# First feed-forward of a two-block kernel: every input weight group stationary, the first two taken by turns for each piece of x

## The chip, the cores and the metric

One NeuronCore of a Trainium2 chip runs the whole kernel. The metric is the device time of one execution in microseconds; lower is better. Everything is fp32. Matrix products are split into high and low parts (`hi*hi + hi*lo + lo*hi`, parts rounded to the fp32r format), so each weight has to be rounded (`w_hi`) and its remainder taken (`w_lo`) before TensorE (PE) may use it.

## The reference

Two blocks on one sequence of 256 tokens of width 1024. The change touches only the first feed-forward, which stands first in the program:

```python
h = _swiglu(_rms_norm(x, ffn1_pre_norm), ffn1_w_in, ffn1_w_out)
x = x + 0.5 * _rms_norm(h, ffn1_post_norm)

def _swiglu(x, w_in, w_out):
    g, u = jnp.split(x @ w_in, 2, axis=-1)      # w_in: 1024 x 5632
    return (jax.nn.silu(g) * u) @ w_out         # w_out: 2816 x 1024
```

After it come a token mixer, a second feed-forward, two more mixers and a final norm. They are computed as before.

## The kernel before, in words

**Weights.** All weights come as one stream of groups of 128 x 2048 fp32 (1 MB). SyncE (SP) loads each into one of `RING = 6` slots of `raw`, as soon as PE has finished with the slot's old group (`RELEASE`). ScalarE (ACT) rounds a group into `w_hi` (`round_to(n)`: all groups below n). VectorE (DVE) then takes the remainder into `w_lo` (`low_to(n)`), in place of `raw`. DVE can't start on a group before ACT has ended it (`hi_done`), and PE can't before DVE has (`lo_done`).

**First feed-forward, input products.** They are 22 groups. The first four are "straight": x is stationary and 512 weight columns stream, in the layout tokens x columns. The results are transposed afterwards (`hidden_transposes`). `opening()` takes these groups in pieces as they land. The other 18 are "chunks": a group holds 128 gate columns and the 128 up columns that belong to them. The weights are stationary and `xT` streams, 32 matmuls to a chunk, by turns of 512 columns (high and low of x with `w_hi`) and 256 columns (`w_lo`). The result is already transposed. A chunk fills one of two pairs of PSUM banks, `acc[:, c % 2]`, first half gate, second half up.

**What a chunk asks of ACT and DVE.** For chunk n, ACT does in this order: copy half of the gate (`gate_second_part`), round a later weight group, SiLU (`chunk_silu`), copy half of up (`up_second_part`), round the product (`chunk_round`). DVE does: sum the gate, scale it by the row of 1/rms of x (`chunk_gate`), take the remainder of a later weight group (`low_to`), sum up (`chunk_up`, which signals `up_summed`), product, remainder of the product (`chunk_low`). Each engine works strictly in the order written. PE begins chunk c only when `up_summed` says that chunk c - 2, the last user of the banks, is summed. In both engines' code the loop over the chunks decides which weight group is handled beside which chunk.

**Norm of x.** The first norm is applied behind the product. Before, ACT squares x by tokens, DVE takes the reciprocals and makes a diagonal, and PE turns it into the row `rstd0_row`. `rates()` is some small mathematics for the later mixers: 20 columns, 20 instructions of DVE and one exponential of ACT.

**Behind it.** `f1_out` follows on PE without a gap. It begins when the last chunk but one is summed; its second token tile begins when the last one is.

Of the kernel before, what the change touches and what calls it, by code (L numbers as in the profile page):

```python
# [59 lines left out]
ACC_READERS = {"f1_in": "V" * 2, "f1_out": "V", "mix_in": "AVVVVVVVVAAAA", "na_out": "V", "mix_out": "V",  # L60
# [7 lines left out]
FILL_COUNTS = [("f1_in", 2), ("t1", 4), ("rq", 2), ("rk", 2), ("rs", 4), ("rp", 4),  # L68
# [4 lines left out]
SPLIT_COUNTS = [("f1_in", 2), ("t1", 4), ("yret", 4), ("merged", 4), ("t2", 4),  # L73
# [5 lines left out]
WARM = 4  # L79
STRAIGHT, CHUNKS = 4, 18  # L80
CHUNKS_BEFORE = {"f1_in": 0, "f2_in": CHUNKS}
# [5 lines left out]
for _name, _n in STAGES:  # L87
    for _g in range(_n):
        if _name in CHUNKS_BEFORE and _g >= STRAIGHT:
            RELEASE.append(("chunk", CHUNKS_BEFORE[_name] + _g - STRAIGHT + 1))  # L90
# [34 lines left out]
def build(nc, first_in, weights, x_turned_in, x_in, gain0_in, gains, rot_in, colmask_in, dist_in, decay_in, lam_in, bias_in, gate_w_in,  # L125
          gate_b_in, conv_a_in, conv_ab_in, conv_b_in, out):
    with ExitStack() as ctx:
# [68 lines left out]
        gate_c = at("gate_c", [P, 2, S], F32, area + 51200)  # L196
        prod_c = at("prod_c", [P, 2, S], F32, area + 53248)

        warm = at("warm", [P, P + 256], F32, area + 63488)
        rstd0_diag = at("rstd0_diag", [P, T, P], F32, area + 65536)  # L200
        rstd0_row = at("rstd0_row", [P, S], F32, area + 66560)

# [57 lines left out]
        warm_set = sem("warm_set")  # L260
        rstd0_ready = sem("rstd0_ready")
        rstd0_diag_ready = sem("rstd0_diag_ready")
        rstd0_row_full = sem("rstd0_row_full")
        rstd0_row_ready = sem("rstd0_row_ready")
        half_hi, half_lo = sem("half_hi"), sem("half_lo")
# [22 lines left out]
        x_landed = [sem(f"x_landed{t}") for t in range(T)]  # L288
        turned_landed = [sem(f"turned_landed{j}") for j in range(KD // 2)]
        unit_landed = [sem(f"unit_landed{j}") for j in range(2)]  # L290
        unit_hi, unit_lo = sem("unit_hi"), sem("unit_lo")
        first_hi, turned_hi = sem("first_hi"), sem("turned_hi")
        part_landed = [sem(f"part_landed{g}") for g in range(1, 3)]
# [80 lines left out]

        def pair_bank(b):

            return acc[:, b % 4 // 2, b % 2]
# [5 lines left out]
        def _(sp):  # L383
# [14 lines left out]
            for j in range(2):  # L398
                sp.dma_start(raw[:, 0, j * UNIT:(j + 1) * UNIT], first_in[j]).then_inc(unit_landed[j], 16)
            load_turned(1)  # L400
            sp.dma_start(raw[:, 0, 2 * UNIT:].rearrange("p (j n) -> p j n", j=2),
                         first_in[2:4].rearrange("j p n -> p j n")).then_inc(landed[0], 16)
            for j in range(2, KD // 2):
                load_turned(j)
            for g in range(1, 3):
                for half, done in enumerate((part_landed[g - 1], landed[g])):
                    part = slice(half * GROUP // 2, (half + 1) * GROUP // 2)
                    sp.dma_start(raw[:, g, part], weights[g - 1][:, part]).then_inc(done, 16)
            sp.dma_start(raw[:, 3, :], weights[2]).then_inc(landed[3], 16)
            for t in range(T):  # L410
                sp.dma_start(x[:, t], x_in[t * P:(t + 1) * P, :]).then_inc(x_landed[t], 16)
            for g in range(4, RING):
                sp.dma_start(raw[:, g, :], weights[g - 1]).then_inc(landed[g], 16)
            for g in range(RING, NG):
# [3 lines left out]
                sp.dma_start(raw[:, g % RING, :], weights[g - 1]).then_inc(landed[g % RING], 16)  # L418
# [12 lines left out]
        def _(pool):  # L431
# [15 lines left out]
            pool.wait_ge(landed[3], 16)  # L447
            for dst, src in ((colmask, colmask_in), (conv_a, conv_a_in), (conv_ab, conv_ab_in),
                             (conv_b, conv_b_in), (gate_b, gate_b_in), (rot, rot_in)):
                pool.dma_start(dst[:], src).then_inc(consts_in, 16)  # L450
            pool.dma_start(logit[:, 0:2 * RH], decay_in.partition_broadcast(P)).then_inc(consts_in, 16)
            pool.dma_start(logit[:, 2 * RH:], lam_in).then_inc(consts_in, 16)
# [18 lines left out]
            def mask_bias(s):  # L471
                pool.wait_ge(bias_in_s[s % 2], 16 * (s // 2 + 1))
                if s == 0:
                    pool.wait_ge(consts_in, 16 * 8)
# [39 lines left out]
        def _(act):  # L514
# [69 lines left out]
            def opening():  # L584

                def token_sums(t):
                    act.wait_ge(x_landed[t], 16)
                    step(a.activation(prod[:].rearrange("p a t n -> p (a t n)"), x[:, t], ACT.Square,
                                      accum_out=sumsq[:, 2 + t:3 + t]))
                    a.activation(std[:, 2 + t:3 + t], sumsq[:, 2 + t:3 + t], ACT.Sqrt, bias=eps1[:], scale=1.0 / DM)\  # L590
                        .then_inc(pre_std, 1)

# [7 lines left out]
                def round_unit(j):  # L600
                    act.wait_ge(unit_landed[j], 16)
                    part = slice(j * UNIT, (j + 1) * UNIT)
                    a.activation(w_hi[:, 0, part], raw[:, 0, part], ACT.Copy).then_inc(unit_hi, 1)

                def round_half(g, half):
                    part = slice(half * GROUP // 2, (half + 1) * GROUP // 2)
# [17 lines left out]
                for t in range(T):  # L624
                    token_sums(t)
# [362 lines left out]
        def _(dve):  # L988
# [150 lines left out]
            def swiglu(which):  # L1139
# [64 lines left out]
                if g0 == 0:  # L1204
                    rates()
# [1018 lines left out]
```

## Time and profile before

| | |
|---|---|
| median of 3 runs | 888.8 us (888.74 to 888.95) |
| the profiled execution's own time | 888.69 us, span 887.0 us |
| PE busy | 879.6 us, 99% |
| DVE, ACT busy | 625.0 us (70%), 489.4 us (55%) |
| granted TensorE clock, mean | 0.999 of 2.4 GHz |
| DMA | 169.89 MB, mean 192 GB/s |

The span runs from the first to the last instruction; the 1.7 us that the execution's own time has more lie around it. In the trace, matmul rows start at even steps when PE is full, so the distance between two starts is the time of what lies between them.

### The profile page before, as it was taken

The numbers are of one execution on the slowest core, as the hardware profiler recorded it, in microseconds if no ns is written. First come the engines' busy times: TensorE is split into PE (matmuls) and PEld (weight loads), VectorE is DVE, ScalarE is ACT, GpSimd is POOL, SyncE is SP. The second block draws the span as 40 slices with busy tenths as digits, with TensorE's granted clock in tenths as the row PEclk, the third lists the DMA queues.
The fourth block names the chain that finished last, engine by engine and source line by source line (L and its number), as shares of the span: only waits on it lengthen the run. The fifth ranks groups of instructions, "written<-read, shape, count | busy, mean of one in ns | idle before, by whom it ended". The sixth has DMA issues, their size and how long they took to land.

```text
span 887.0 us, 11473 instructions
## 1 busy us (share of the span) xinstructions
PE 879.6 (99%) x4628; PEld 752.3 (85%) x4628; DVE 625.0 (70%) x808; ACT 489.4 (55%) x661; POOL 64.4 (7%) x89
## 2 busy tenths in 40 slices
PE   9999999999999999999999999999999999999997
PEld 7888888888888888888888888888999888888886
DVE  6887776467767656577577777446979857888872
ACT  6865564445444556446565555435887644555551
POOL 2000000003021110000000000000390000000000
PEclk9999999999999999999999999999999999999999
DMA  9955555455753444455655555546534456555521
GB/s 352 368 188 191 191 189 199 147 190 179 282 198 127 180 168 173 184 190 190 237 190 190 191 190 190 189 182 251 184 106 181 151 187 254 190 190 191 190 95 48
DMA packets 26948, 169.89 MB, mean 192 GB/s; under 512 B 3616, under 2 KB 3664, under 8 KB 7952
## 3 DMA queue, kind: packets, MB, share of 16 engines
q1 hardware_dynamic: 24368, 161.23, 50.3%
q0 software_dynamic: 2240, 7.66, 2.5%
q8 instruction: 37, 0.61, 0.3%
q10 hardware_dynamic: 288, 0.27, 0.1%
q14 instruction: 15, 0.12, 0.0%
HBM read 167.05 MB, written 1.05 MB: 190 GB/s over the span
## 4 chain that ended last, share of the span: by engine, by line
PE 97%; DVE 1%; ACT 1%; issue 0%; ACTq 0%
PE acc L1839 15%; PE acc L1642 15%; PE acc L1640 15%; PE acc L1641 15%; PE acc L2101 8%; PE acc L1841 7%; PE acc L2103 4%; PE acc L1655 2%; PE acc L1883 2%; PE acc L2053 2%; PE acc L2054 2%; PE acc L2052 2%; PE aux L2037 1%; PE aux L1764 1%; PE acc L1885 1%; PE aux L1641 1%
## 5 line engine op out<-in xcount | busy, mean ns | idle before, releaser
L996 DVE TENSOR_TENSOR w_lo<-raw,w_hi 128x2048 fp32r<-128x2048 f32 x147 | 336.8, 2300 | 89.9 <-ACT w_hi L522 89.5
L522 ACT ACTIVATE w_hi<-raw 128x2048 fp32r<-128x2048 f32 x145 | 275.7, 1911 | 62.6 <-DMA raw<-weights 62.4
L1839 PE MATMUL acc<-xT,w_hi 128*128 128x512 f32 x576 | 200.4, 394 | 0.0
L1841 PE MATMUL acc<-xT,w_lo 128*128 128x256 f32 x576 | 159.7, 277 | 0.0
L1839 PEld LDWEIGHTS acc<-xT,w_hi 128*128 128x128 f32 x576 | 108.0, 188 | 25.0
L1640 PE MATMUL acc<-w_hi,xT 128*128 128x512 f32 x312 | 124.0, 398 | 0.0
L1642 PE MATMUL acc<-w_hi,xT 128*128 128x512 f32 x312 | 121.8, 390 | 0.0
L1641 PE MATMUL acc<-w_lo,xT 128*128 128x512 f32 x312 | 121.5, 390 | 0.0
L2101 PE MATMUL acc<-xT,w_hi 128*128 128x512 f32 x320 | 111.3, 394 | 0.0
L1841 PEld LDWEIGHTS acc<-xT,w_lo 128*128 128x128 f32 x576 | 108.2, 188 | 0.0
L2103 PE MATMUL acc<-xT,w_lo 128*128 128x256 f32 x320 | 88.7, 277 | 0.0
L2101 PEld LDWEIGHTS acc<-xT,w_hi 128*128 128x128 f32 x320 | 60.0, 188 | 13.8
L1642 PEld LDWEIGHTS acc<-w_hi,xT 128*128 128x128 f32 x312 | 58.6, 188 | 12.6
L1640 PE MATMUL acc<-w_hi,hT_hi 128*128 128x512 f32 x176 | 68.7, 390 | 0.0
L1640 PEld LDWEIGHTS acc<-w_hi,xT 128*128 128x128 f32 x312 | 58.6, 188 | 11.8 <-issue 0.6
L1642 PE MATMUL acc<-w_hi,hT_lo 128*128 128x512 f32 x176 | 68.5, 389 | 0.0
L1641 PE MATMUL acc<-w_lo,hT_hi 128*128 128x512 f32 x176 | 68.5, 389 | 0.0
L1641 PEld LDWEIGHTS acc<-w_lo,xT 128*128 128x128 f32 x312 | 58.7, 188 | 11.4
L2103 PEld LDWEIGHTS acc<-xT,w_lo 128*128 128x128 f32 x320 | 60.1, 188 | 0.0
L677 ACT ACTIVATE hT_hi<-prod_c 128x256 fp32r<-128x256 f32 x36 | 15.1, 418 | 43.4 <-DVE prod_c L1182 43.4
L1640 PEld LDWEIGHTS acc<-w_hi,hT_hi 128*128 128x128 f32 x176 | 33.0, 188 | 6.9
L1641 PEld LDWEIGHTS acc<-w_lo,hT_hi 128*128 128x128 f32 x176 | 33.0, 188 | 6.8
(263 smaller groups left out, 1290.4 us busy)
## 6 DMA issues: line engine op xcount, KB each, us to landing
raw<-weights SPq DMA_DIRECT2D x147, 1024.0 KB, 4.8
gain_pre<-gains POOLq DMA_DIRECT2D x5, 512.0 KB, 5.0
raw<-weights SPq DMA_DIRECT2D x4, 512.0 KB, 7.5
gain_post<-gains POOLq DMA_DIRECT2D x3, 512.0 KB, 5.6
gate_w<-gate_w_in POOLq DMA_DIRECT2D x1, 1536.0 KB, 8.5
x_turned<-x_turned_in SPq DMA_DIRECT2D x4, 256.0 KB, 4.9
x<-x_in SPq DMA_DIRECT2D x2, 512.0 KB, 11.6
bias_raw<-bias_in POOLq DMA_DIRECT2D x16, 64.0 KB, 3.2
```

Source lines behind the costliest of these rows:

```text
L522: a.activation(w_hi[:, g % RING], raw[:, g % RING], ACT.Copy).then_inc(hi_done, 1)
L996: v.tensor_tensor(w_lo[:, slot], raw[:, slot], w_hi[:, slot].bitcast(F32), ALU.subtract)\
L1640: m.matmul(dst, hi[:, k, cols], w_hi[:, slot, w], start=first, stop=False)
L1641: m.matmul(dst, hi[:, k, cols], w_lo[:, slot, w], start=False, stop=False)
L1642: return m.matmul(dst, lo[:, k, cols], w_hi[:, slot, w], start=False, stop=last)
L1655: i = m.matmul(acc[:, t, column], xT[:, k, t * P:(t + 1) * P], w[:, g, unit * UNIT:(unit + 1) * UNIT], start=k == 0 and xT is xT_hi and w ...
L1839: m.matmul(dst, w_hi[:, slot, w], xT[:, k].rearrange("p a q -> p (a q)"), start=k == 0, stop=False)
L1841: i = m.matmul(dst[:, 0:S], w_lo[:, slot, w], xT[:, k, 0], start=False, stop=k == KD - 1)
L1883: m.matmul(dst, w_hi[:, g % RING, w], xT[:, k].rearrange("p a q -> p (a q)"), start=k == 0, stop=False)
L2052: m.matmul(dst, w_hi[:, slot, w], xT_hi[:, k, :], start=k == 0, stop=False)
L2101: m.matmul(dst, w_hi[:, g % RING, w], xT[:, k].rearrange("p a q -> p (a q)"), start=k == 0, stop=False)
L2103: i = m.matmul(dst[:, 0:S], w_lo[:, g % RING, w], xT[:, k, 0], start=False, stop=k == KD - 1)
```

## The change

All 22 groups of the first feed-forward become chunks. Chunks 0 and 1 are fed by turns with each quarter of x as it lands; chunks 2 and 3 go to the four `aux` banks, so that nothing waits for `acc` at first. `gate_c` and `prod_c` become four buffers deep. The transposes of the straight groups fall away. The sum of squares of x comes from the transposed x: ACT squares it, DVE folds eight parts into one, PE sums over the partitions with a matrix of ones, ACT takes the root as a row, DVE the reciprocal of the row (`rstd0_row`, 128 x 256); PE turns it back for the norm behind. `rates()` is cut in four and put into chunks 6, 8, 10 and 12. The second feed-forward keeps four straight groups.

```diff
-WARM = 4
-STRAIGHT, CHUNKS = 4, 18
+STRAIGHT = {"f1_in": 0, "f2_in": 4}
+CHUNKS = {name: FF // P - n for name, n in STRAIGHT.items()}
...
+        def chunk_bank(stage_name, n, half):
+            if stage_name == "f1_in" and n in (2, 3):
+                return aux[:, 2 * (n - 2) + half]
+            return acc[:, n % 2, half]
...
(ACT)
+                if which == "f1":
+                    a.activation(x_squares[:].rearrange("p k q -> p (k q)"), x_turned[:].rearrange("p j e q -> p (j e q)"),
+                                 ACT.Square).then_inc(squares_ready, 1)
+                    split[0] = 3
+                    round_to(4)
+                    for n in range(2):
+                        gate_second_part(n)
+                        up_second_part(n)
+                    act.wait_ge(sums0_full, 1)
+                    a.activation(std0_row[:], aux[:, 2, 0:S], ACT.Sqrt, bias=eps1[:], scale=1.0 / DM).then_inc(pre_std, T)
+                    round_to(5)
+                    gate_second_part(2)
+                    up_second_part(2)
+                    chunk_silu(0)
+                    chunk_silu(1)
+                    round_to(6)
+                    chunk_round(0)
+                    chunk_round(1)
+                    chunk_silu(2)
+                    gate_second_part(3)
+                    up_second_part(3)
+                    round_to(7)
+                    chunk_round(2)
+                    chunk_silu(3)
+                    chunk_round(3)
...
-                for n in range(CHUNKS):
+                for n in range(0 if straight else 4, chunks):
                     gate_second_part(n)
-                    round_to(g0 + 8 + n)
+                    round_to(g0 + straight + n + 4)
                     chunk_silu(n)
                     up_second_part(n)
...
                     chunk_round(n)
+                    if not straight and n == 6:
+                        act.wait_ge(ls_neg, 1)
+                        a.activation(ls[1][:], ls[0][:], ACT.Exp).then_inc(ls_exp, 1)
...
(DVE)
+                if which == "f1":
+                    dve.wait_ge(squares_ready, 1)
+                    step(v.tensor_tensor(x_squares[:, 0:4], x_squares[:, 0:4], x_squares[:, 4:8], ALU.add))
+                    step(v.tensor_tensor(x_squares[:, 0:2], x_squares[:, 0:2], x_squares[:, 2:4], ALU.add))
+                    v.tensor_tensor(sums0[:], x_squares[:, 0], x_squares[:, 1], ALU.add).then_inc(sums0_ready, 1)
+                    low_to(4)
+                    for n in range(2):
+                        step(gate_sum(n))
+                        chunk_up(n)
+                    dve.wait_ge(pre_std, T)
+                    v.reciprocal(rstd0_row[:], std0_row[:]).then_inc(rstd0_row_ready, 1)
+                    dve.wait_ge(rstd0_row_ready, 1)
+                    gate_scale(0)
+                    gate_scale(1)
+                    low_to(5)
...
+                    low_to(7)
+                    chunk_low(2)
+                    chunk_product(3)
+                    chunk_low(3)
...
-                for n in range(CHUNKS):
+                for n in range(0 if straight else 4, chunks):
                     chunk_gate(n)
-                    low_to(g0 + 7 + n)
+                    low_to(g0 + n + (7 if straight else 4))
                     chunk_up(n)
...
+                    if not straight and n == 8:
+                        rates_ratio()
+                    if not straight and n == 10:
+                        rates_series()
+                    if not straight and n == 12:
+                        rates_end()
...
(PE, in chunk(c))
-                    pe.wait_ge(lo_done, g0 + STRAIGHT + c + 1)
-                    if c < 2:
+                    pe.wait_ge(lo_done, g0 + straight + c + 1)
+                    if straight and c < 2:
                         pe.wait_ge(acc_free_dve[c], n_dve + 2)
+                    elif not straight and c == 3:
+                        pe.wait_ge(pre_std, T)
+                    elif not straight and c < 6:
+                        pe.wait_ge(up_summed, c - 3)
                     else:
                         pe.wait_ge(up_summed, c_before + c - 1)
```

**The loop on ACT.** Before, in chunk 1 (the second of the 18), ACT's instructions stand as follows; `landed2` is the arrival of group 8:

```order
L662 ACTIVATE gate_c<-acc 128x256 [waits gate_chunk_full]
L522 ACTIVATE w_hi<-raw 128x2048 [waits landed2]
L672 ACTIVATE gate_c<-gate_c 128x256 [waits gate_summed]
L667 ACTIVATE prod_c<-acc 128x256 [waits chunk_full]
L677 ACTIVATE hT_hi<-prod_c 128x256 [waits prod_ready]
L662 ACTIVATE gate_c<-acc 128x256 [waits chunk_lo,gate_chunk_full]
```

In the changed kernel chunk 4, the first of the loop, reads alike; `landed1` is the arrival of group 7:

```order
L666 ACTIVATE gate_c<-acc 128x256 [waits chunk_lo,gate_chunk_full]
L535 ACTIVATE w_hi<-raw 128x2048 [waits landed1]
L676 ACTIVATE gate_c<-gate_c 128x256 [waits gate_summed]
L671 ACTIVATE prod_c<-acc 128x256 [waits chunk_full]
L681 ACTIVATE hT_hi<-prod_c 128x256 [waits prod_ready]
L666 ACTIVATE gate_c<-acc 128x256 [waits chunk_lo,gate_chunk_full]
```

The order within a chunk has not moved. Both times ACT rounds the group of the chunk three further on.

**The loop on DVE.** Before, in the same chunk 1; the `w_lo` row is group 7, which ACT rounded one chunk earlier:

```order
L1167 TENSOR_TENSOR gate_c<-acc,gate_c 128x256 [waits gate_part]
L1168 TENSOR_TENSOR gate_c<-gate_c,rstd_row 128x256 [waits dve_step]
L996 TENSOR_TENSOR w_lo<-raw,w_hi 128x2048 [waits hi_done]
L1176 TENSOR_TENSOR prod_c<-acc,prod_c 128x256 [waits up_part]
L1182 TENSOR_TENSOR prod_c<-prod_c,gate_c 128x256 [waits up_summed,silu_ready]
L1188 TENSOR_TENSOR hT_lo<-prod_c,hT_hi 128x256 [waits chunk_hi]
```

In the changed kernel, chunks 4 (its last five rows) and, with the series of `rates`, chunk 10. In chunk 4 the `w_lo` row is group 7, the very group that ACT rounds in chunk 4:

```order
L1200 TENSOR_TENSOR gate_c<-gate_c,rstd_row 128x256 [waits dve_step]
L1018 TENSOR_TENSOR w_lo<-raw,w_hi 128x2048 [waits hi_done]
L1213 TENSOR_TENSOR prod_c<-acc,prod_c 128x256 [waits up_part]
L1220 TENSOR_TENSOR prod_c<-prod_c,gate_c 128x256 [waits up_summed,silu_ready]
L1226 TENSOR_TENSOR hT_lo<-prod_c,hT_hi 128x256 [waits chunk_hi]
```

```order
L1018 TENSOR_TENSOR w_lo<-raw,w_hi 128x2048 [waits hi_done]
L1213 TENSOR_TENSOR prod_c<-acc,prod_c 128x256 [waits up_part]
L1160 SCALAR_TENSOR_TENSOR ls_69<-ls_69,ls_68 128x20
L1160 SCALAR_TENSOR_TENSOR ls_69<-ls_69,ls_68 128x20 [waits dve_step] x6
L1220 TENSOR_TENSOR prod_c<-prod_c,gate_c 128x256 [waits up_summed,silu_ready,dve_step]
L1226 TENSOR_TENSOR hT_lo<-prod_c,hT_hi 128x256 [waits chunk_hi]
```

The rows read alike but are shifted against ACT's: DVE's group is now the one that ACT handles in the same chunk, not the one of the chunk before. The small mathematics, which stood ahead of the loop, now stands between the sum of up and the product.

**The start on DVE.** In the changed kernel these rows follow the remainders of the first three groups:

```order
L1231 TENSOR_TENSOR x_squares<-x_squares 128x1024 [waits squares_ready]
L1232 TENSOR_TENSOR x_squares<-x_squares 128x512 [waits dve_step]
L1233 TENSOR_TENSOR sums_98<-x_squares 128x256 [waits dve_step]
L1018 TENSOR_TENSOR w_lo<-raw,w_hi 128x2048 [waits hi_done]
L1196 TENSOR_TENSOR gate_c<-acc,gate_c 128x256 [waits gate_part]
L1213 TENSOR_TENSOR prod_c<-acc,prod_c 128x256 [waits up_part,dve_step]
L1196 TENSOR_TENSOR gate_c<-acc,gate_c 128x256 [waits gate_part]
L1213 TENSOR_TENSOR prod_c<-acc,prod_c 128x256 [waits up_part,dve_step]
L1239 RECIPROCAL rstd_row<-std_row 128x256 [waits pre_std]
```

The folding of the squares, the sums of chunks 0 and 1 and the wide reciprocal are new here; before, two reciprocals of one column and two small diagonals stood in this place.

## Rows read from the trace of the kernel before

**Rows 1.** The page: busy time of each engine; the chain that ended last, by engine.

```profile
PE 879.6 (99%) x4628; PEld 752.3 (85%) x4628; DVE 625.0 (70%) x808; ACT 489.4 (55%) x661; POOL 64.4 (7%) x89
...
PE 97%; DVE 1%; ACT 1%; issue 0%; ACTq 0%
```

**Rows 2.** Timeline of PE: start us, us busy, engine, line, operation, operands, shapes, count.

```profile
14.63 1.98 PE L1655 MATMUL acc<-w_hi,xT 128*128 128x512 f32 x8
...
17.35 1.98 PE L1655 MATMUL acc<-w_hi,xT 128*128 128x512 f32 x8
...
28.70 0.60 PE L1821 MATMUL aux<-ident,prod 128*128 128x128 f32 x4
29.05 0.48 PE L1839 MATMUL acc<-xT,w_hi 128*128 128x512 f32 x1
...
46.32 0.39 PE L1839 MATMUL acc<-xT,w_hi 128*128 128x512 f32 x1
...
129.52 0.39 PE L1640 MATMUL acc<-w_hi,hT_hi 128*128 128x512 f32 x1
```

**Rows 3.** Timeline of ACT, one chunk, in brackets idle before and releaser.

```profile
45.45 0.42 ACT L677 ACTIVATE hT_hi<-prod_c 128x256 fp32r<-128x256 f32 x1 [1.71 <-DVE prod_c L1182]
45.78 0.37 ACT L662 ACTIVATE gate_c<-acc 128x256 f32<-128x256 f32 x1
46.04 1.91 ACT L522 ACTIVATE w_hi<-raw 128x2048 fp32r<-128x2048 f32 x1
47.85 0.41 ACT L672 ACTIVATE gate_c<-gate_c 128x256 f32<-128x256 f32 x1
48.15 0.38 ACT L667 ACTIVATE prod_c<-acc 128x256 f32<-128x256 f32 x1
```

**Rows 4.** Timeline of DVE, the same chunk.

```profile
46.25 0.42 DVE L1167 TENSOR_TENSOR gate_c<-acc,gate_c 128x256 f32<-128x256 f32 x1
46.70 0.43 DVE L1168 TENSOR_TENSOR gate_c<-gate_c,rstd_row 128x256 f32<-128x256 f32 x1
47.04 2.28 DVE L996 TENSOR_TENSOR w_lo<-raw,w_hi 128x2048 fp32r<-128x2048 f32 x1
49.24 0.42 DVE L1176 TENSOR_TENSOR prod_c<-acc,prod_c 128x256 f32<-128x256 f32 x1
49.77 0.43 DVE L1182 TENSOR_TENSOR prod_c<-prod_c,gate_c 128x256 f32<-128x256 f32 x1
50.68 0.42 DVE L1188 TENSOR_TENSOR hT_lo<-prod_c,hT_hi 128x256 fp32r<-128x256 f32 x1 [0.48 <-ACT hT_hi L677]
```

**Rows 5.** Timeline of DVE, four chunks later.

```profile
66.35 0.42 DVE L1167 TENSOR_TENSOR gate_c<-acc,gate_c 128x256 f32<-128x256 f32 x1 [0.69 <-ACT gate_c L662]
```

**Rows 6.** Timeline of ACT, start of the program.

```profile
14.67 1.06 ACT L608 ACTIVATE w_hi<-raw 128x1024 fp32r<-128x1024 f32 x1 [0.21 <-DMA raw<-weights]
17.17 1.92 ACT L522 ACTIVATE w_hi<-raw 128x2048 fp32r<-128x2048 f32 x1 [1.45 <-DMA raw<-weights]
...
30.22 1.28 ACT L696 ACT_TABLE_LOAD   x1
```

**Rows 7.** Timeline of DVE, start of the program: remainders of 512 and 1024 columns.

```profile
5.37 0.68 DVE L1085 TENSOR_TENSOR w_lo<-raw,w_hi 128x512 fp32r<-128x512 f32 x1
...
9.04 1.23 DVE L1012 TENSOR_TENSOR w_lo<-raw,w_hi 128x1024 fp32r<-128x1024 f32 x1 [0.92 <-ACT w_hi L608]
```

**Rows 8.** Timeline of DVE, the small mathematics.

```profile
32.38 0.18 DVE L1125 TENSOR_SCALAR ls<-ls 128x20 f32<-128x20 f32 x1 [0.29 <-ACT ls L696]
...
33.54 1.46 DVE L1131 SCALAR_TENSOR_TENSOR ls<-ls,ls 128x20 f32<-128x20 f32 x7
```

**Rows 9.** Groups of DVE by form: busy us, mean ns, idle before.

```profile
L1106 DVE RECIPROCAL rstd<-std 128x1 f32<-128x1 f32 x2 | 0.3, 160 | 0.4 <-ACT std L590 0.4
L1126 DVE RECIPROCAL ls<-ls 128x20 f32<-128x20 f32 x1 | 0.3, 278 | 0.0
```

**Rows 10.** End of the program: busy time by engine, granted clock, DMA share, GB/s.

```profile
880.00:887.00 7.00, 1.29 (x6) 0.75 (x4) 2.04 (x4) 1.83 (x4) 0.00 (x0) 0.82 0.20 75
```

More of the change, by code:

```diff
@@ L613, in opening, with round_half @@
                 act.wait_ge(gain0_landed, 16)
-                x_hi(1)
-                round_half(0, 1)
-                x_hi(2)
-                x_hi(3)
-                round_half(1, 0)
-                round_half(1, 1)
+                for j in range(1, 4):
+                    x_hi(j)
+                    round_both(j)
                 round_half(2, 0)
                 round_half(2, 1)
-                split[0] = 3
-                round_to(4)
-                for t in range(T):
-                    token_sums(t)
+            def round_half(g, half):
+                part = slice(half * GROUP // 2, (half + 1) * GROUP // 2)
+                act.wait_ge(landed[g] if half else part_landed, 16)
+                a.activation(w_hi[:, g, part], raw[:, g, part], ACT.Copy).then_inc(hi_done if half else half_hi, 1)
             act.dma_start(gain0[:], gain0_in).then_inc(gain0_landed, 16)
@@ L1141, in swiglu @@
                 st = f"{which}_in"
[L1142 to L1143 removed]
+                g0, f0, q0 = FIRST_GROUP[st], FIRST_FILL.get(st), FIRST_SPLIT.get(st)
+                gate0 = GATES_F2
                 def up(j, par, t):
@@ new lines, in weight, with long_products, short_products @@
+                def weight(slot, w, k, half):
+                    return w[:, slot, 2 * P * k + P * half:2 * P * k + P * (half + 1)]
+                def long_products(c, ks):
+                    for half in range(2):
+                        for k in ks:
+                            m.matmul(chunk_bank("f1_in", c, half), weight(c, w_hi, k, half), xT[:, k].rearrange("p a q -> p (a q)"),
+                                     start=k == 0, stop=False)
+                def short_products(c, ks):
+                    for half in range(2):
+                        for k in ks:
+                            i = m.matmul(chunk_bank("f1_in", c, half)[:, 0:S], weight(c, w_lo, k, half), xT_hi[:, k],
+                                         start=False, stop=k == KD - 1)
+                        if ks[-1] == KD - 1:
+                            i.then_inc(chunk_full if half else gate_chunk_full, 1)
@@ new lines, in opening @@
+                pe.wait_ge(zeros_set, 1)
+                for half in range(2):
+                    m.matmul(acc[:, 0, half], zeros[:, 0:P], zeros[:], start=True, stop=False)
+                pe.wait_ge(unit_hi, 1)
+                pe.wait_ge(first_hi, 1)
+                for half in range(2):
+                    for k in range(2):
+                        m.matmul(acc[:, 0, half, 0:S], weight(0, w_hi, k, half), xT_hi[:, k], start=False, stop=False)
+                pe.wait_ge(xn_ready, 1)
+                for half in range(2):
+                    for k in range(2):
+                        m.matmul(acc[:, 0, half, S:2 * S], weight(0, w_hi, k, half), xT_lo[:, k], start=False, stop=False)
@@ new lines, in opening @@
+                pe.wait_ge(half_hi, 1)
+                long_products(2, range(0, 4))
+                pe.wait_ge(half_lo, 1)
+                short_products(2, range(0, 4))
+                pe.wait_ge(dve_ones_set, 1)
+                pe.wait_ge(sums0_ready, 1)
+                m.matmul(aux[:, 2, 0:S], ones[:], sums0[:], start=True, stop=True).then_inc(sums0_full, 1)
+                pe.wait_ge(hi_done, 3)
+                long_products(2, range(4, 8))
+                pe.wait_ge(lo_done, 3)
+                short_products(2, range(4, 8))
```

391 lines of the change are left out of this document (182 added, 209 removed).

## The prediction, made before the changed kernel ran

> **What bounds the kernel now.** First I read the page's busy times and chain: PE is busy for 99% of the span and makes 97% of the chain, DVE stands at 70%, ACT at 55% [rows 1]. So only two things can move the time: fewer microseconds of PE's own work, or a new wait of PE. Next the timeline of PE through the first feed-forward [rows 2]. It shows no gap: the first two groups are used up at 17.35, chunk 3 starts at 46.32, `f1_out` at 129.52. From 46.32 to 129.52 there are 15 chunks, so a chunk takes PE 5.547 us. Last the timelines of ACT and DVE for one chunk [rows 3, 4], because the change reorders those. The reader should see that DVE is the slower of the two and that it is behind PE there: it never waits for PE, its chunk ends with a wait of 0.48 for ACT's rounding of the product, and its next one would start 0.34 later, at 51.02. That is 4.77 us after 46.25. Since 4.77 is less than 5.547, DVE catches up, and four chunks later it waits 0.69 for PE's results [rows 5]. This margin of 0.78 us a chunk is what the change spends.
>
> **PE's own work.** It is nearly unchanged. A chunk streams 16 x 768 columns and a straight group 24 x 512, which is the same number. The opening takes the same bytes in another order, behind a warming-up of the same size. I let chunks 0 and 1 end at 17.35, where the first two groups end now [rows 2]. Two sets of four transposes go (0.35 us each, from 28.70 to 29.05, [rows 2]) and the diagonal product; the sum over partitions comes (256 columns in fp32, near those 0.35: I take 0.4), and the turning back of the row (two products of one column, between nothing and 0.35: I take 0.2). Alone, PE would reach `f1_out` at 17.35 + 0.4 + 20 x 5.547 + 0.2 = 128.9, which is 0.6 us earlier than 129.52. This is all that the change can win here.
>
> **Step 1: the start of DVE.** Chunk 6 reuses the banks of chunk 4, so it waits for the sum of chunk 4's up half. When does DVE get there? ACT starts its last piece of group 2 at 14.67 and can issue the next after 0.96; the squares (2048 columns, 1.91 as the rounding of 2048 in [rows 3]) end at 17.54. The three foldings of 1024, 512 and 256 columns take 1.26 + 0.72 + 0.34 start to start, with 1.23 and 0.68 from [rows 7]: 19.89. From here DVE never rests, since ACT is done with group 3 before 19.9 (group 3 landed at 17.17, [rows 6]). Start to start, a remainder takes 2.20, an instruction of 256 columns 0.34, or 0.45 where the next one needs it [rows 4]:
> - group 3, then two gate sums and two up sums: 2.20 + 1.58 = 23.67
> - the wide reciprocal: the trace has none. A reciprocal of 1 column takes 0.160 and of 20 columns 0.278 [rows 9], 0.0062 us a column, so 256 columns make 1.74. Bounds: not under the 0.42 of any instruction of this width [rows 4]. With the handover, 25.44
> - two scalings 0.68, group 4 2.20: 28.32; gate and up of chunk 2, products 0 and 1, 1.81: 30.13; group 5: 32.33; two remainders, gate and up of chunk 3, product 2, 2.15: 34.48; group 6 and a remainder: 37.02
> - product 3 starts, 0.46 to ACT's rounding, 0.33 to the gate copy of chunk 4: 37.81; 0.26 to the rounding of group 7, 1.94 until DVE may start on it, 2.20 and the sum of up, 0.42: 42.63.
>
> PE is ready for chunk 6 at 17.35 + 0.4 + 4 x 5.547 = 39.95. It waits 2.7 us.
>
> **Step 2: the loop.** From chunk 4 on DVE takes the remainder of the very group that ACT rounds in the same chunk; before, ACT was one group ahead. Both queues are in order, so one chunk becomes a closed ring: gate copy to rounding 0.26, rounding 1.91, handover 0.03, remainder to sum of up 2.20, to the product 0.53, to its rounding on ACT 0.46, to the next gate copy 0.33 [rows 3, 4]. (The handover: 49.77 + 0.43 + 0.42 and two of them make 50.68.) The ring is 5.72 us. Four buffers don't open it, since no wait of it is one for a buffer. PE needs 5.547, so it now follows the ring, with a wait of about 0.17 in each chunk. `f1_out` starts after the sum of chunk 20: 16 rings behind that of chunk 4, 42.63 + 91.5 = 134.1.
>
> **Step 3: the small mathematics.** Before, it ran ahead of the loop, while DVE's delay still fitted into PE's first chunk. Now it sits inside the ring, between the sum of up and the product. It starts 0.34 after the sum instead of the product's 0.53, so 0.19 of each piece is covered. An instruction takes 0.213 (seven are busy for 1.46, and a handover of 0.03 to the next, [rows 8]). The four pieces cost 0.24, 0.97 (1.16 from 32.38 to 33.54, [rows 8]), 1.30 and 6 x 0.213 - 0.19 = 1.09. The exponential on ACT stands between two chunks: a table load of 1.28 [rows 6] and 0.12, 1.40. The load back to SiLU is covered: rounding 1.80, load 1.28, SiLU and up copy 0.6 are 3.7, and the ring has 1.94 + 2.20 there. Together 5.0.
>
> **The sum.** `f1_out` starts at 134.1 + 5.0 = 139.1 or so, against 129.52: +9.6. Its second token tile waits for the last chunk, one ring of 5.72 later, while the first tile takes 24 x 0.227 = 5.45 (12 matmuls of 512 columns from 14.63 to 17.35, [rows 2]): +0.3. Behind it nothing is changed; weights are long there, and the second feed-forward keeps its lead of one group. So +9.9 on the profiled execution's 888.69 us (the median is 888.8): **898.6 us**. Unknown terms: the reciprocal -1.3 to +0.5; handovers of the ring 0.05 either way, 16 times, 0.8; DMA in pieces of 2 KB instead of 4 KB in the opening, 0 to +1, as every step hangs on the end of group 2. Its own range is 896.5 to 900.9.
>
> **The rivals.**
> - *PE never waits; not slower.* The ring would have to be 0.17 us shorter, and DVE 2.7 us earlier at chunk 4. For it speaks that PE is the bound nearly everywhere [rows 1] and that the margin missing per chunk is small. Against it: all lengths of the ring are from rows of the same instructions. 888.69 - 0.6 = 888.1 us.
> - *Only the first wait stays* (the ring falls under 5.547 but the start doesn't mend): 2.7 - 0.6, 890.8 us.
> - *The ring binds but the mathematics is covered* by slack that I don't see: 898.6 - 5.0 = 893.6 us.
> - *TensorE's clock falls in the new waits.* In the last 7 us of the program, with PE busy for only 1.29, the mean granted clock is 0.82 [rows 10]; over the whole program it is 0.999. If chunk 6 ran at 1.2 GHz, it would end 5.5 us later, but the steps of 5.72 and the 5.0 of mathematics give PE that time back before it counts. Two chunks in a row at 1.2 GHz would cost some 4 us: 902.6 us. Against it: the longest wait is 2.7 us, the others 0.17 to 1.6.
>
> The Trainium skill (TensorE: Matmul & The Clock Gate, "HAM oscillation") warns of just this, a clock that falls in the waits between blocks of matmuls and is paid for again each time. [...] The waits that I work out are short beside the end of the program, the only place where the trace shows a fall.
>
> **Chances.** My forecast 0.78, PE never waits 0.10, only the first wait 0.04, mathematics covered 0.03, clock 0.05. The range 893 to 902 us holds nearly all of the forecast's cases, the covered mathematics and a part of the clock's: about 0.81. A measurement here tells 0.2%, 1.8 us, from no change. Slower by more: all but the first rival, 0.90. Of its 0.10, at 888.1, I give 0.07 to the same and 0.03 to faster.
>
> **What would show it.** In the profile after: a wait of some 2.7 us before chunk 6 with the sum of up (DVE `prod_c`) as releaser; before each later chunk one of about 0.17, more at chunks 9, 11, 13 and 15 (about 1.0 to 1.8); DVE's remainders of weights, idle before each for about 0.9, released by ACT's `w_hi`; an `f1_out` at about 139; the same distances from there on. Wrong it would be if PE shows no wait in the chunks, if DVE's loop repeats in less than 5.55, if the wide reciprocal takes far from 1.74, or if ACT's queue is ahead of DVE's by more than the order shows.

## The result and the profile after

The changed kernel takes 900.27 us (median of 4 runs, 899.73 to 900.78), the kernel before 888.88 us beside it (4 runs, 888.74 to 889.59). The ratio is 1.0118, with a 95% interval from 1.0105 to 1.0131: slower by 11.4 us, of which 9.9 were forecast. The profiled execution took 900.42 us, with a span of 898.7.

First the page, busy times and the chain that ended last, then two of its groups of instructions:

```profile
PE 885.9 (99%) x4654; PEld 755.1 (84%) x4654; DVE 633.1 (70%) x824; ACT 488.4 (54%) x666; POOL 64.4 (7%) x89
...
PE 87%; DVE 7%; ACT 4%; issue 1%; DMA 1%; SPq 1%; DVEq 0%; ACTq 0%
...
L1018 DVE TENSOR_TENSOR w_lo<-raw,w_hi 128x2048 fp32r<-128x2048 f32 x147 | 336.9, 2300 | 100.4 <-ACT w_hi L535 100.0
...
L1920 PE MATMUL acc<-xT,w_hi 128*128 128x512 f32 x576 | 205.8, 402 | 5.0 <-DVE prod_c L1213 5.0
```

Busy shares tell nearly nothing: PE has 99% as before [rows 1]. The chain tells it. PE's share fell from 97% to 87%, and DVE and ACT now hold 11%: for about 100 us the end is set by a loop that goes through them. The waits that the group of PE's chunks reports are only 5.0 us; where the rest of the 11.4 is, the timelines have to say.

The timeline of PE, at the landmarks of [rows 2]; in brackets the idle time before and its releaser:

```profile
17.78 2.00 PE L1723 MATMUL aux<-xT,w_hi 128*128 128x512 f32 x8
...
20.58 0.60 PE L1773 MATMUL aux<-sums,ones 128*128 128x256 f32 x2
20.82 2.19 PE L1723 MATMUL aux<-xT,w_hi 128*128 128x512 f32 x8
...
42.93 0.47 PE L1920 MATMUL acc<-xT,w_hi 128*128 128x512 f32 x1 [2.00 <-DVE prod_c L1213]
...
44.52 0.63 PE L1920 MATMUL acc<-xT,w_hi 128*128 128x512 f32 x1
44.94 0.41 PE L1922 MATMUL acc<-xT,w_lo 128*128 128x256 f32 x1
45.16 0.63 PE L1920 MATMUL acc<-xT,w_hi 128*128 128x512 f32 x1
...
74.09 0.47 PE L1920 MATMUL acc<-xT,w_hi 128*128 128x512 f32 x1 [0.89 <-DVE prod_c L1213]
...
86.82 0.47 PE L1920 MATMUL acc<-xT,w_hi 128*128 128x512 f32 x1 [1.12 <-DVE prod_c L1213]
...
99.32 0.47 PE L1920 MATMUL acc<-xT,w_hi 128*128 128x512 f32 x1 [0.99 <-DVE prod_c L1213]
...
139.25 0.50 PE L1711 MATMUL acc<-w_hi,hT_hi 128*128 128x512 f32 x1
```

`f1_out` starts at 139.25, 9.73 later than before. The first wait has the place and the releaser that the prediction gave it. The sum over partitions took 0.24 (20.58 to 20.82). And between 44.52 and 45.16 something is odd: a pair of matmuls takes 0.64 us, where it takes 0.35 elsewhere. The windows of one microsecond (busy time of PE, PEld, DVE, ACT, POOL, the granted clock, DMA share, GB/s) say what it is:

```profile
43.00:44.00 1.00, 1.00 (x6) 0.86 (x7) 0.51 (x2) 0.66 (x3) 0.00 (x0) 1.00 0.96 401
44.00:45.00 1.00, 1.00 (x6) 0.85 (x5) 0.97 (x3) 1.00 (x2) 0.00 (x0) 0.64 0.95 401
45.00:46.00 1.00, 1.00 (x5) 0.90 (x4) 0.15 (x2) 1.00 (x2) 0.00 (x0) 0.50 0.11 33
...
48.00:49.00 1.00, 1.00 (x8) 0.86 (x6) 0.90 (x3) 0.00 (x0) 0.00 (x0) 1.00 0.00 0
```

After the wait of 2.00 us PE ran at full clock for 1.4 us, then at 1.2 GHz from about 44.3 to 47.7, and then at 2.4 GHz again. Six pairs took 3.65 us there (44.06 to 47.71) in place of 2.08: 1.6 us lost in the first chunk behind the wait. This is the rival "TensorE's clock falls" come true, in a smaller size than it was priced. It also took the place of a wait: of the four that were forecast at chunks 9, 11, 13 and 15 the first is missing, as PE was late itself there (it started chunk 9 at 61.72, 0.17 after the sum that it needs had ended), and the other three stand above. The Trainium skill (TensorE: Matmul & The Clock Gate, "HAM oscillation") warns of a clock that falls in waits between blocks of matmuls and is paid for again each time; the waits in its own case, 3 to 5 us for data, are longer than any here. In this trace the clock fell behind the wait of 2.00 us and behind none of the later ones, up to 1.12 us long.

DVE, the same stretch as [rows 4]:

```profile
23.86 1.74 DVE L1239 RECIPROCAL rstd_row<-std_row 128x256 f32<-128x256 f32 x1
...
44.59 0.42 DVE L1200 TENSOR_TENSOR gate_c<-gate_c,rstd_row 128x256 f32<-128x256 f32 x1
45.87 2.29 DVE L1018 TENSOR_TENSOR w_lo<-raw,w_hi 128x2048 fp32r<-128x2048 f32 x1 [0.85 <-ACT w_hi L535]
48.08 0.41 DVE L1213 TENSOR_TENSOR prod_c<-acc,prod_c 128x256 f32<-128x256 f32 x1
48.59 0.42 DVE L1220 TENSOR_TENSOR prod_c<-prod_c,gate_c 128x256 f32<-128x256 f32 x1
49.51 0.42 DVE L1226 TENSOR_TENSOR hT_lo<-prod_c,hT_hi 128x256 fp32r<-128x256 f32 x1 [0.48 <-ACT hT_hi L681]
...
66.85 0.42 DVE L1213 TENSOR_TENSOR prod_c<-acc,prod_c 128x256 f32<-128x256 f32 x1
67.19 0.17 DVE L1151 TENSOR_SCALAR ls<-ls 128x20 f32<-128x20 f32 x1
...
68.34 0.43 DVE L1220 TENSOR_TENSOR prod_c<-prod_c,gate_c 128x256 f32<-128x256 f32 x1
```

The row to compare is `w_lo`. In [rows 4] it followed the scaling at once, as ACT had long been done with its group. Now 0.85 us of idling stand before it, released by ACT. And this is the closed ring at work on ACT, where the same chunk begins:

```profile
43.34 0.42 ACT L681 ACTIVATE hT_hi<-prod_c 128x256 fp32r<-128x256 f32 x1 [2.65 <-DVE prod_c L1220]
43.67 0.37 ACT L666 ACTIVATE gate_c<-acc 128x256 f32<-128x256 f32 x1
43.93 1.90 ACT L535 ACTIVATE w_hi<-raw 128x2048 fp32r<-128x2048 f32 x1
```

ACT's rounding of the product waits for DVE, the rounding of the group stands behind it in the queue, and DVE waits for that: 43.93 + 1.90 and a handover of 0.04 give 45.87. The whole of DVE's waits from 38 to 140 us in two rows (total us, times, longest; a third, one wait of 1.4 for ACT's `gate_c`, is left out):

```profile
DVE w_lo L1018 <- ACT w_hi L535: 14.6, 17, 0.9
DVE hT_lo L1226 <- ACT hT_hi L681: 8.2, 17, 0.5
```

The sum of up starts at 42.37, 48.08, 53.79, 61.13, 66.85, 73.53, 79.25, 86.26, 91.98 and 98.76, and then every 5.7 us to the end. So one chunk takes 5.71 or 5.72, and the four with a piece of the small mathematics 1.63, 0.97, 1.30 and 1.07 more: together 4.97.

### The profile page after: what moved, and what is told of

It reads as the page before. It is cut to its first block, busy times and chain, and to the rows that moved or that the text cites. A ratio compares the mean times of both kernels' runs of the same rounds, so it can differ in the third digit from the quotient of the medians.

```text
span 898.7 us, 11544 instructions
## 1 busy us (share of the span) xinstructions
PE 885.9 (99%) x4654; PEld 755.1 (84%) x4654; DVE 633.1 (70%) x824; ACT 488.4 (54%) x666; POOL 64.4 (7%) x89
## 4 chain that ended last, share of the span: by engine, by line
PE 87%; DVE 7%; ACT 4%; issue 1%; DMA 1%; SPq 1%; DVEq 0%; ACTq 0%
PE acc L1711 15%; PE acc L1713 15%; PE acc L1712 15%; PE acc L1920 11%; PE acc L2186 8%; PE acc L1922 5%; PE acc L2188 4%; DVE w_lo L1018 4%; ACT w_hi L535 2%; PE acc L1968 2%; PE acc L2138 2%; PE acc L2139 2%; PE acc L2137 2%; PE aux L2122 1%; PE aux L1841 1%
## 5 line engine op out<-in xcount | busy, mean ns | idle before, releaser
L1920 PE MATMUL acc<-xT,w_hi 128*128 128x512 f32 x576 | 205.8, 402 | 5.0 <-DVE prod_c L1213 5.0
L1711 PE MATMUL acc<-w_hi,xT 128*128 128x512 f32 x304 | 120.7, 397 | 0.0
L1713 PE MATMUL acc<-w_hi,xT 128*128 128x512 f32 x304 | 118.7, 390 | 0.0
L1712 PE MATMUL acc<-w_lo,xT 128*128 128x512 f32 x304 | 118.4, 390 | 0.0
L2186 PE MATMUL acc<-xT,w_hi 128*128 128x512 f32 x320 | 111.3, 394 | 0.0
L1713 PEld LDWEIGHTS acc<-w_hi,xT 128*128 128x128 f32 x304 | 57.1, 188 | 12.2
L1711 PEld LDWEIGHTS acc<-w_hi,xT 128*128 128x128 f32 x304 | 57.2, 188 | 11.5 <-issue 0.6
L1713 PEld LDWEIGHTS acc<-w_hi,hT_lo 128*128 128x128 f32 x176 | 33.0, 188 | 6.9
```

Of the source, the lines that this page charges most:

```text
L1711: m.matmul(dst, hi[:, k, cols], w_hi[:, slot, w], start=first, stop=False)
L1712: m.matmul(dst, hi[:, k, cols], w_lo[:, slot, w], start=False, stop=False)
L1713: return m.matmul(dst, lo[:, k, cols], w_hi[:, slot, w], start=False, stop=last)
L1920: m.matmul(dst, w_hi[:, slot, w], xT[:, k].rearrange("p a q -> p (a q)"), start=k == 0, stop=False)
L2186: m.matmul(dst, w_hi[:, g % RING, w], xT[:, k].rearrange("p a q -> p (a q)"), start=k == 0, stop=False)
```

## The experiments

The theory: the ring costs the time. It closes because both engines handle the same group in the same chunk; it costs its excess over PE's 5.547 us a chunk, the late start, and all small work put into it. The rivals: the late start and the mathematics alone; the clock; the deeper buffers, or what lies behind `f1_out`. Kernels are compared with the kernel before on the same chip.

**One group of lead for ACT.**

```diff
-                    round_to(g0 + straight + n + 4)
+                    round_to(g0 + straight + n + (4 if straight else 5))
```

> The changed kernel, but ACT rounds one weight group more in chunk 4 and is one group ahead of DVE from there on; nothing else. Theory 'ring' (ACT's rounding and DVE's remainder of the same group stand in one closed ring of 5.72 us a chunk): DVE's waits of 0.85 us for w_hi in the chunks go, its loop falls to 4.77 us, PE keeps only the wait of about 2 us before chunk 6 and meets no other; f1_out starts at about 131.5 to 132.5 instead of 139.25, the time falls by some 7 to 8 us to 892.5 to 893.5. Rival 'start and mathematics' (what costs is DVE's late start and the mathematics in the loop, the ring is not what holds PE): under 3 us of gain, since neither is touched. For the second feed-forward, which this edit doesn't touch, both leave its matmul pace open.

Measured: 894.05 us against 889.31, ratio 1.0053 (1.0038 to 1.0069), so 6 us of the 11.4 are back. That is a little less than the 7 to 8 expected, and twice the rival's 3. The profiled execution took 892.87. DVE's timeline:

```profile
45.19 0.42 DVE L1200 TENSOR_TENSOR gate_c<-gate_c,rstd_row 128x256 f32<-128x256 f32 x1
45.53 2.28 DVE L1018 TENSOR_TENSOR w_lo<-raw,w_hi 128x2048 fp32r<-128x2048 f32 x1
47.73 0.42 DVE L1213 TENSOR_TENSOR prod_c<-acc,prod_c 128x256 f32<-128x256 f32 x1
```

The wait before `w_lo` is gone, and a chunk of DVE takes 4.77 (scaling to scaling, 45.19 to 49.96), exactly what it took before. So the ring is what one group of lead opens. PE's waits from 5 to 150 us:

```profile
PE acc L1920 <- DVE prod_c L1213: 2.2, 1, 2.2
PE acc L1723 <- ACT w_hi L617: 1.4, 1, 1.4
```

One wait in the chunks is left, 2.16 us at chunk 6, and one of 1.38 in the opening, where the changed kernel had 0.3; `f1_out` starts at 132.80, 0.3 above the range expected, and the longer wait in the opening is enough for that. The mathematics, which is still in the loop, costs nothing here, as DVE has 0.78 us a chunk to spare again: its price is a price of the closed ring.

This run also speaks on the clock. In the microsecond from 45 to 46, 2 us behind its wait, it shows

```profile
45.00:46.00 1.00, 1.00 (x8) 0.87 (x7) 0.97 (x3) 1.00 (x1) 0.00 (x0) 1.00 0.50 197
```

the full clock, after a wait longer than that of the changed kernel. The median lies 1.2 us above the profiled execution. A clock that falls in other executions would make 1.6 us of it, since here PE is the bound again and nothing hides the loss. That is not shown: the mean granted clocks of the four executions were 0.999 at 892.87 us, 0.998 at 893.89, 1.000 at 894.22 and 0.996 at 895.36. The slowest may have had such a fall; the one of 894.22 had not, and was 1.3 us slower than the profiled one all the same.

**The small mathematics out of the loop.** The four pieces on DVE and the exponential on ACT go behind it:

```diff
-                    if not straight and n == 6:
-                        rates_begin()
...
-                    if not straight and n == 12:
-                        rates_end()
...
+                if not straight:
+                    rates_begin()
+                    rates_ratio()
+                    rates_series()
+                    rates_end()
```

> The changed kernel, but all four pieces of the small mathematics and the exponential stand behind the loop over the chunks, ahead of the weights of f1_out; the ring stays. Theory 'ring': each piece costs its length less 0.19 us, together 5.0 us, so f1_out starts at 134.3 and the time is 895.3 us, and PE still waits about 0.17 us in every chunk. Rival 'the pieces are covered' (DVE has 0.85 us of idle time in each chunk, which takes them up): less than 2 us of gain.

Measured: 895.19 us, ratio 1.0067 (1.0049 to 1.0085), profiled execution 894.72. `f1_out`:

```profile
134.46 0.40 PE L1708 MATMUL acc<-w_hi,hT_hi 128*128 128x512 f32 x1
```

That is 4.79 earlier than in the changed kernel, where the sum of the steps was 5.0. The wait before chunk 6 is 2.23, at 42.97, and the clock stayed at 1.00 behind it too. The rival that DVE's idle time covers the pieces (under 2 us) falls. This run alone can't tell the ring from a price that the mathematics has wherever it stands; with the run before, it is a term only as long as the ring is closed.

**DVE one group behind ACT.** The ring can be opened from the other side too. DVE leaves out one remainder ahead of the loop and is a group later from then on, which also takes 2.2 us out of its late start:

```diff
-                    low_to(7)
...
-                    low_to(g0 + n + (7 if straight else 4))
+                    low_to(g0 + n + (7 if straight else 3))
```

> The changed kernel, but DVE takes the remainder of each weight group one chunk later: the remainder of group 6 moves from ahead of chunk 4 into chunk 4, and so on. ACT is untouched. Theory 'ring': this opens the ring as well and in addition brings the sum of chunk 4 forward by 2.2 + 0.86 us, so PE doesn't wait before chunk 6 either; f1_out at 129.9 to 130.7, time 889.2 to 892 us, by the matmul pace. Rival 'start and mathematics': the wait before chunk 6 goes (2.0 us), the mathematics still costs 5 us, 896 to 898 us.

Measured: 890.38 us (10 runs, 889.35 to 891.18), ratio 1.0006 (0.9997 to 1.0016). PE's waits from 5 to 150 us are a single row:

```profile
PE acc L1722 <- ACT w_hi L617: 0.7, 1, 0.7
```

It is in the opening. No chunk waits any more, `f1_out` starts at 130.10. With one call left out and one constant changed, nearly all 11 us are gone. Taken with the first run: `f1_out` is 2.70 earlier than there, of which 2.16 are the wait at chunk 6, the late start; the rest is about what the opening waited less (0.7 for 1.4). The medians lie 3.7 apart; where the last 1.0 is, no profile says.

**The kernel before with buffers four deep.** Does depth cost or give anything?

```diff
-        gate_c = at("gate_c", [P, 2, S], F32, area + 51200)
-        prod_c = at("prod_c", [P, 2, S], F32, area + 53248)
+        gate_c = at("gate_c", [P, 4, S], F32, area + 51200)
+        prod_c = at("prod_c", [P, 4, S], F32, area + 55296)
...
-                    if n >= 2:
-                        act.wait_ge(chunk_lo, c_before + n - 1)
-                    a.activation(gate_c[:, n % 2], ...
+                    if n >= 4:
+                        act.wait_ge(chunk_lo, c_before + n - 3)
+                    a.activation(gate_c[:, n % 4], ...
```

> The kernel before, but gate_c and prod_c four buffers deep in both feed-forwards; nothing else of the change. In the changed kernel the matmul pairs of the second feed-forward's chunks came 353.3 ns apart, before 346.7 ns (1.7 us over the stage), with no waits. Theory 'buffers' (other addresses or the looser wait make PE's pairs slower): the second feed-forward shows 353 ns here too, and the time is 1.5 to 2 us (in both stages up to 3.7 us) above the kernel before. Rival 'phase' (PE's loads and matmuls lock into one of two paces, by nanoseconds of how the stream starts, whatever the code): the time of the kernel before within 0.1 us, or a slow pace in one stage and not the other.

Measured: 889.25 us, ratio 0.9999 (0.9990 to 1.0009), `f1_out` at 129.97. Nothing either way, with the ring open as it is in this kernel. That four buffers don't open a closed ring is seen in the changed kernel itself, which has them. The 1.7 us that the second feed-forward lost (next) don't come with the buffers here either.

**What the second feed-forward lost.** Its code is unchanged, and yet its 18 chunks end 11.7 us later than before, not 10. The timeline of PE at `f2_out`, before:

```profile
537.87 0.39 PE L1640 MATMUL acc<-w_hi,hT_hi 128*128 128x512 f32 x1
```

and after:

```profile
549.59 0.40 PE L1711 MATMUL acc<-w_hi,hT_hi 128*128 128x512 f32 x1
```

PE never waits there, in either kernel, and the clock is 1.00. Its groups of instructions from 460 to 530 us (count, busy us, mean ns) differ all the same, before:

```profile
L1839 PE MATMUL acc<-xT,w_hi 128*128 128x512 f32 x203 | 70.4, 394 | 0.0
```

and after:

```profile
L1920 PE MATMUL acc<-xT,w_hi 128*128 128x512 f32 x199 | 70.4, 399 | 0.0
L1922 PE MATMUL acc<-xT,w_lo 128*128 128x256 f32 x199 | 55.9, 281 | 0.0
```

In the same 70 us PE has done 4 pairs less. The pair of 512 and 256 columns has two paces: 394 ns for the wide one stands for starts 346.7 ns apart, 399 ns for 353.3. A chunk of 16 pairs takes 5.547 or 5.653. Chunk 0 had the slow pace before and the fast one after, chunks 1 to 17 the fast one before and the slow one after: 17 x 0.106 less 0.106, 1.7 us. What stands between chunks 0 and 1 is four transposes. New theory: a run of chunks keeps its pace, and only something else between two pairs can flip it. The rival: the changed kernel's other addresses or timing of DMAs slow PE's pairs.

**The same kernel once more**, unedited, for a second profile:

> The changed kernel once more, unedited, for a second profile. Theory 'phase': f1_out again at 139.2 within 0.4; the pairs of the second feed-forward at 353 or at 347 ns, and the time 1.7 us less if at 347. Rival 'code' (something in the changed code makes that stage slow): 353 ns again.

It took 898.97 us. Its group of the same 70 us:

```profile
L1920 PE MATMUL acc<-xT,w_hi 128*128 128x512 f32 x203 | 70.4, 394 | 0.0
```

The pace is the fast one, and `f2_out` starts at 548.15, although `f1_out` was later (139.55) than in the first profile. So the pace isn't a property of the kernel: the same program has run at both. Its waits before chunks were 1.99, 0.76, 1.13 and 0.89, and its clock fell behind the first of them again:

```profile
44.00:45.00 1.00, 1.00 (x5) 0.82 (x4) 0.97 (x3) 1.00 (x2) 0.00 (x0) 0.50 1.05 442
```

**The transposes moved.** The kernel before, with the four transposes of the second token tile, and their copies, three chunks later in both stages:

```diff
-                    if n == 0:
+                    if n == 3:
                         hidden_hi(1, 1)
...
-                    if c == 0:
+                    if c == 3:
```

> The kernel before, but the second set of hidden transposes, with its copy on ACT and its remainder on DVE, stands behind chunk 3 instead of chunk 0, in both feed-forwards. Theory 'phase' (a run of matmul pairs keeps one of two paces until something interrupts it): the pairs of chunks 1, 2 and 3 come 353 ns apart like those of chunk 0, those behind the transposes 347 ns; about +0.3 us in each stage. Rival 'place' (the first chunk is slow for a reason of its own, such as full DMA queues or what ACT and DVE do then): chunks 1 to 3 at 347 ns, no change of time.

Measured: 889.98 us (10 runs), ratio 1.0009 (0.9999 to 1.0018). PE's groups in the second feed-forward, chunks 0 to 3, and then behind the transposes:

```profile
L1839 PE MATMUL acc<-xT,w_hi 128*128 128x512 f32 x49 | 17.4, 399 | 0.0
...
L1839 PE MATMUL acc<-xT,w_hi 128*128 128x512 f32 x50 | 17.5, 395 | 0.0
```

The slow pace now lasts as long as the transposes are put off, and ends behind them; the first feed-forward shows the same (399 ns from 29.5 to 46 us, 394 from 53 to 70). The rival with addresses falls, here as in the run before: no address and no DMA instruction is other. The moments at which DMAs ran in each execution were not tried by themselves. In the second feed-forward the four transposes changed the pace in every profile at the full clock, from slow to fast in nine and from fast to slow in two (this is why the first profile of the changed kernel lost there); chunk 0 already has the one or the other.

**Both moves**, the later DVE and the mathematics behind the loop:

> The changed kernel with both moves: DVE takes the remainders of the weight groups one chunk later, and the small mathematics stands behind the loop. Theory 'ring': with the ring open the mathematics was already covered, so nothing is won over the kernel with the first move alone: 890.4 us within 0.7, ratio to before 1.000 to 1.002. Rival 'the mathematics costs of itself': up to 5 us below that, 885.5 us.

Measured: 889.43 us (11 runs), ratio 1.0001 (0.9992 to 1.0009), against 889.36. `f1_out` starts at 129.88, and PE waits nowhere from 10 us to 150. This is a little better than expected, and equal to the kernel before.

**An interruption on purpose.** The kernel with the later DVE runs chunks 2 to 5 at the slow pace. Two matmuls of one column ahead of chunk 3, whose results nobody uses:

```diff
+                        if c == 3:
+                            for _ in range(2):
+                                m.matmul(aux[:, 3, 0:1], ones[:], zeros[:, 0:1], start=True, stop=True)
```

> The kernel with DVE's remainders one chunk later, and in addition two products of one column, whose result nobody reads, ahead of chunk 3. Theory 'phase': the pairs of chunks 3 to 5, 353 ns without them, come 347 ns apart; 0.3 us less, 0.2 us for the products themselves. Rival 'place': 353 ns up to chunk 6 as before the edit, and 0.1 to 0.2 us more.

Measured: 889.49 us, ratio 1.0001 (0.9991 to 1.0010). Its profiled execution ran at a mean granted clock of 0.655 and took 1255 us, so that it says nothing on the pace, and the kernel was run once more for a profile:

> The kernel with DVE's remainders one chunk later and two idle products of one column ahead of chunk 3, once more, for a profile with the clock at full speed. Theory 'phase': pairs of chunks 3 to 5 at 347 ns. Rival 'place': 353 ns up to chunk 6.

It took 890.84 us, `f1_out` started at 130.02. Groups of PE from 25 to 43 us, without the two products:

```profile
L1919 PE MATMUL acc<-xT,w_hi 128*128 128x512 f32 x39 | 13.8, 399 | 0.0
```

and with them:

```profile
L1919 PE MATMUL acc<-xT,w_hi 128*128 128x512 f32 x39 | 13.6, 394 | 0.0
```

Chunk 2, ahead of the products, has no such pairs (its matmuls come eight of a width in a row), so that no flip is seen within one trace. But chunks 3 to 5 ran at the slow pace in all six profiles of the changed kernel and its variants without the products, and at the fast one in both with them (this one and the next run's). `f1_out` came 0.08 us earlier, which is nothing beside what the opening varies. And neither kind of break steers the pace for good: the two products of one column ahead of chunk 7, which turn the row back, left it fast in these two profiles and turned it from fast to slow in the second profile of the changed kernel, and the second feed-forward ran at 399 ns in this execution and at 394 in the next run's.

**All three edits together**, the candidate for a kernel that beats both:

> The changed kernel with DVE's remainders one chunk later, the small mathematics behind the loop and the two idle products ahead of chunk 3: the best that the experiments point to. Theory 'PE bound' (with every new wait gone, only PE's own work is left, 0.6 us less than before by the sum, less what the start of the program varies): f1_out at 129.3 to 129.7, 888.6 to 889.3 us, ratio to before 0.999 to 1.000. Rival 'gain held back' (the whole of a hidden gain comes out once nothing waits): under 887.5 us.

Measured: 889.34 us (12 runs, 888.83 to 891.15) against 889.61, ratio 0.9992 (0.9980 to 1.0004), `f1_out` at 129.98, later than the 129.3 to 129.7 expected. Not distinguishable from the kernel before. The first rival of the prediction gave 888.1 for a PE that never waits; with every wait gone PE ends where it ended before, so the 0.6 us that stood in that sum aren't there.

## Why the prediction was right, point by point

- **What bounds the kernel, and the margin of 0.78 us.** Right. Of the two runs with one group of lead, one has DVE's chunk at 4.77 and the other no wait in the chunks at all.
- **PE's own work.** Slightly too good. The first two groups ended at 17.78, not 17.35; the sum over partitions took 0.24, not 0.4; chunk 2, whose matmuls come eight of a width in a row, took 5.78 (17.78 to 23.80 without the sum), and chunks 3 to 5 ran at the slow pace, 5.65, all for 5.547: together 0.55 more. By the starts of its pairs PE was ready for chunk 6 at 40.77, where 39.95 was worked out, so it stood for 2.16 and not 2.7; the row says 2.00, as the last record's end is drawn 0.16 later. The turning back of the row took 0.37 (50.17 to 50.54), not 0.2. None of this moved the end, since DVE decided.
- **Step 1, the start of DVE.** Right: the sum of up of chunk 4 ended at 42.79 (42.37 and 0.42), 0.16 later than the 42.63 worked out, and chunk 6 began at 42.93. The wide reciprocal, a value extended from 1 and 20 columns to 256, took 1.74 us, as worked out from [rows 9].
- **Step 2, the ring.** Right, in place, releaser and size: 5.71 to 5.72 for 5.72, an idling of 0.85 for 0.9. The waits of 0.17 a chunk are there, but no row calls them idle: PE's chunks start at 110.78, 116.48, 122.20, 127.91 and 133.63, 5.70 to 5.73 apart, and what is over stands in the first one or two pairs of a chunk, 0.40 to 0.44 us each for 0.35. From 42.93 to 139.25 PE took 96.3 us for 16 chunks of 5.547, 7.6 more than its own work at the fast pace: 3.5 in the waits at chunks 11, 13 and 15 (by starts 1.04, 1.28 and 1.15, inside the 1.0 to 1.8 that was to be seen; the rows say 3.0 together), 1.6 by the clock, 0.4 in the turning back of the row, and the other 2.1 in such stretched pairs and the slow pace of some chunks.
- **Step 3, the mathematics.** 4.97 for 5.0; taken out, 4.79 came back. The single pieces were 1.63, 0.97, 1.30 and 1.07 for 1.64, 0.97, 1.30 and 1.09.
- **The sum to `f1_out`.** +9.73 for +9.6, and the second token tile +0.38 for +0.3 (the first transposes of the norm behind it came 10.11 later). This is the prediction's +9.9 with 0.2 more.
- **"Behind it nothing is changed."** This step failed. It is true of the instructions and not of the time: in the first profile the second feed-forward took 1.7 us more by its pace. The second profile of the same kernel, at the fast pace, took 898.97 us, 0.4 above the forecast. Whether the unprofiled runs, around 900.3, all had the slow pace is open.
- **The rivals.** That PE never waits, that only the first wait stays, and that the mathematics is covered fell with the ring. The clock did fall, at 1.2 GHz for 3.4 us behind the wait of 2.00, and cost 1.6 us of PE's time; as the prediction worked out for one chunk, the steps of the ring gave it back before it counted: the sums of up go on at 5.71 right through it.

## What to carry to other kernels

When two engines with queues in order handle the same item in the same turn of a loop (one rounds it, the other takes the remainder), and the second also feeds the first, their instructions form a ring: add up its length from the timelines of both and compare it with the bounding engine's turn. Here it was 5.72 against 5.547; one item of lead, given by one constant, made it 4.77, and buffers four deep did not open it. Small work placed inside such a ring costs its full length less the slack at that one place (4.97 us here, where 5.0 were worked out), and nothing once the ring is open; and a kernel bound by one engine gains no more from lost waits than that engine's waits, which were none before the change.

## What the runs showed of the hardware

- A stream of pairs of matmuls of 512 and 256 columns has two paces at the full granted clock, 346.7 and 353.3 ns a pair, and in these traces mostly holds one until transposes, products of one column or a wait come between. Four transposes changed it each time in the second feed-forward (eleven profiles); products of one column and waits sometimes changed it and sometimes did not (it stayed slow behind the wait of 2.23 us, and turned fast behind that of 2.16). The same kernel ran 17 chunks at the one and at the other. What decides the pace was not tried and stays open.
- The granted clock fell to 1.2 GHz behind a wait of 2.0 us in both profiles of the changed kernel, beginning not in the wait but 1.4 us (about 0.3 in the second profile) after matmuls had resumed, and stayed at 2.4 GHz behind waits of 2.16 and 2.23 us in two others. So the length of this one wait does not decide it, and what does is open.
- A reciprocal of 256 columns took 1.74 us, of 1 column 0.160: 6.2 ns for each further column. An operation on two inputs took 0.42 us for 256 columns and 2.28 for 2048: 1.04 ns for each further column.
